# A hybrid decoder trunk: the first FFN by Strassen's method too, and the second layer's modulation on GpSimd

## The chip, the cores and the metric

The kernel runs on one core of one Trainium2 chip. The metric is the device time of one execution in microseconds; a figure for a kernel is the median of several runs. One execution is also taken by the hardware profiler, and its records are the trace that the sections below read. Five engines work side by side: TensorE (PE; PEld is its weight load), VectorE (DVE), ScalarE (ACT), GpSimd (POOL) and SyncE (SP), each with its own queue of instructions that it takes in order. They wait for each other by semaphores only.

## What is computed

A trunk of two residual layers over 512 tokens of 1024 channels, all in float32. Each layer has a mixer and a SwiGLU FFN, both behind an RMS norm that is shifted, scaled and gated by a modulation vector computed from `c`:

```python
h = x
c_act = silu(c)
for i in range(2):
    mod = c_act @ ada_w[i] + ada_b[i]              # 1024 x 6144, six parts of 1024
    sh_m, sc_m, gt_m, sh_f, sc_f, gt_f = split(mod, 6)
    hn = rms_norm(h, norm_mix_w[i]) * (1 + sc_m) + sh_m
    y = even_mixer(hn, ...) if i == 0 else odd_mixer(hn, ...)
    h = h + gt_m * y
    hn = rms_norm(h, norm_ffn_w[i]) * (1 + sc_f) + sh_f
    gate, up = split(hn @ ffn_w_in[i], 2)          # 1024 x 5632
    h = h + gt_f * ((silu(gate) * up) @ ffn_w_out[i])   # 2816 x 1024
return rms_norm(h, final_norm_w)
```

The even mixer is a gated DeltaNet beside an S5 state-space layer; the odd one is stick-breaking attention with eight heads.

## The kernel before

The activations stay in SBUF, channels on the partitions, 512 tokens along the free axis. Every weight is loaded by SyncE into one of two `raw` buffers, split into a high and a low part (ScalarE writes `whi`, L1535 and L1939; VectorE writes `wlo` = `raw` - `whi`, L2144), and multiplied in three passes (`pass3`, L622 to L624), high by high, high by low, low by high. A load of weights with its products is called a slot; slots alternate between the two buffers, so that a slot's `wlo` must be there before TensorE begins it.

**FFN of layer 0 (FFN0).** 2816 hidden channels are 22 tiles, in two halves of 12 and 10. A plain slot makes one tile: the gate block and the up block, 8 k-tiles by 3 passes each, 48 matmuls of 512 columns. ScalarE takes the Silu of the gate, VectorE multiplies (L2620) and splits into `ff_hi` and `ff_lo`. After each half eight out blocks multiply by `ffn_w_out`, and VectorE adds each, gated, to `h` (L2574).

**FFN of layer 1 (FFN1).** 22 tiles in thirds of 8, 8 and 6. The first four are plain slots, the other 18 Strassen slots: the tokens and the gate and up columns are each halved, and seven products of half the size (`half_product`, L1365 to L1367; 4 k-tiles by 3 passes, 256 columns) replace eight, 84 matmuls in all. VectorE makes sums of weight quarters for this (`sum_full`, L2830 to L2839, and their low part, L2847) and puts the corners together again (L2854, L2860, L2871). Four sums of activation quarters, the T tiles, are made once, before the first of these slots. Eight out blocks follow each third.

**The modulation.** Part p of layer i is `c_act @ ada_w[i]` over 1024 columns, taken as 8 tiles of 128 rows by 1024 columns: a tile is multiplied by one column of `c_act` (a scalar on each partition) and added to an accumulator. VectorE then folds the accumulator over the partitions in part, and TensorE ends it (`folded_parts`). Layer 0's fifth part (`scale_acc`) is done largely on GpSimd by a tensor_scalar (L3100) and a tensor_tensor (L3101) a tile, beside VectorE's products of the S5 output gate (`y_s`, L2519). Layer 0's last part, the FFN's gate, is 8 tiles on VectorE, two ahead of FFN0 and six within it. Layer 1's 48 tiles are done by VectorE within FFN0, three parts at a time, one scalar_tensor_tensor of 128x3072 behind a hidden tile (L2634), on loads that GpSimd's queue issues (L3121).

**What sets the order.** Nothing is scheduled by a program: each engine's instructions stand in the order in which the code is written, and the waits on semaphores do the rest. Between FFN0 and the attention stands `late_norm(2, ...)`, the norm of the attention's input; it needs the last out block, and TensorE's first product of the attention needs it.

Of the kernel before, what the change touches and what calls it, by code (L numbers as in the profile page):

```python
# [3159 lines left out]
```

## Time and profile before

| | |
|---|---|
| median of 3 runs | 1302.54 us (1300.65 to 1304.43) |
| the profiled execution's own time | 1305.82 us |
| its span, first to last instruction | 1304.2 us |
| mean granted TensorE clock, share of full speed | 0.986 |
| busy: PE, DVE, ACT, POOL | 1260.0, 864.0, 582.7, 181.0 us |

Busy time is an average over stages with different limits, so the stages are read one by one: FFN0 lies from about 349 to 699 us of the span, the norm behind it to 724, the attention to about 935, FFN1 to the end. A row of the timeline is one instruction, with its start and its duration; an engine that has to wait for another has in brackets how long it stood idle and what released it. An instruction whose operands are kept from it while it already runs has no such bracket: it is only longer.

### The profile page before, as it was taken

To read this page: it belongs to the slowest core of one execution; us is meant where nothing else is said; L and a number is where in the kernel's file an instruction comes from. 1 tells how busy PE (TensorE), PEld (TensorE's weight loads), DVE (VectorE), ACT (ScalarE), POOL (GpSimd) and SP (SyncE) were. 2 spreads that over 40 slices of the span, in tenths; PEclk is the share of its full clock that TensorE was granted. 3 is DMA by queue.
4 is the path that set the end of the run, shared out by engine and by line. 5 is a ranking of instruction groups with operands and counts; after the bars stand their busy time and mean duration, and the time that the engine had idled before them with its cause. 6 is when DMAs were issued, how large, how long until landed. Compare 5 with 4: busy or idle time off the path is not lost.

```text
span 1304.2 us, 19810 instructions
## 1 busy us (share of the span) xinstructions
PE 1260.0 (97%) x7915; PEld 1073.5 (82%) x7915; DVE 864.0 (66%) x1045; ACT 582.7 (45%) x747; POOL 181.0 (14%) x242
## 2 busy tenths in 40 slices
PE   5999999899999999999999999999999999999997
PEld 3588788788788888888888888887879989988995
DVE  3799976567876663466467466455789458846865
ACT  6444752444432222222334476556575335523543
POOL 4007964930000000000000000000500000000000
PEclk8999999989999999999999999999999999999999
DMA  9593625425248763377233221112232243325212
GB/s 338 160 145 122 188 76 154 140 86 173 66 122 286 232 222 105 112 241 240 59 90 129 97 65 65 57 57 81 65 97 82 80 126 101 97 75 146 83 59 90
DMA packets 207475, 163.34 MB, mean 125 GB/s; under 512 B 31790, under 2 KB 197899, under 8 KB 205355
## 3 DMA queue, kind: packets, MB, share of 16 engines
q1 hardware_dynamic: 204496, 137.02, 36.3%
q0 software_dynamic: 2400, 25.20, 5.3%
q8 instruction: 50, 0.82, 0.3%
q14 instruction: 23, 0.18, 0.0%
q10 hardware_dynamic: 506, 0.12, 0.0%
HBM read 157.21 MB, written 4.19 MB: 124 GB/s over the span
## 4 chain that ended last, share of the span: by engine, by line
PE 76%; DVE 9%; POOL 5%; ACT 5%; issue 2%; DMA 1%; ACTq 0%; POOLq 0%; DVEq 0%; SPq 0%
PE banks L622 17%; PE banks L624 17%; PE banks L623 17%; PE banks L1365 5%; PE banks L1367 5%; PE banks L1366 5%; DVE wlo L2144 2%; PE banks L937 2%; PE banks L1272 1%; PE banks L927 1%; PE banks L1234 1%; DVE hn_lo L2194 1%; POOL scan_a L3048 1%; DMA raw<-in_ffn_w_in_dram 1%; DVE tmp L2188 1%
## 5 line engine op out<-in xcount | busy, mean ns | idle before, releaser
L2144 DVE TENSOR_TENSOR wlo<-raw,whi 128x2048 fp32r<-128x2048 f32 (+4 forms) x116 | 229.1, 1976 | 87.5 <-ACT whi L1529 41.4
L622 PE MATMUL banks<-hn_hi,whi 128*128 128x512 f32 x688 | 273.8, 398 | 5.2 <-DVE hn_lo L2292 2.2
L624 PE MATMUL banks<-hn_hi,wlo 128*128 128x512 f32 x688 | 270.2, 393 | 0.0
L623 PE MATMUL banks<-hn_lo,whi 128*128 128x512 f32 x688 | 270.2, 393 | 0.0
L622 PE MATMUL banks<-ff_hi,whi 128*128 128x512 f32 x416 | 163.3, 392 | 0.0
L624 PE MATMUL banks<-ff_hi,wlo 128*128 128x512 f32 x416 | 162.0, 389 | 0.0
L623 PE MATMUL banks<-ff_lo,whi 128*128 128x512 f32 x416 | 162.0, 389 | 0.0
L622 PEld LDWEIGHTS banks<-hn_hi,whi 128*128 128x128 f32 x688 | 130.5, 190 | 36.0 <-DVE hn_lo L2194 3.5
L624 PEld LDWEIGHTS banks<-hn_hi,wlo 128*128 128x128 f32 x688 | 130.4, 190 | 27.7
L623 PEld LDWEIGHTS banks<-hn_lo,whi 128*128 128x128 f32 x688 | 130.7, 190 | 26.2
L1535 ACT ACTIVATE whi<-raw 128x2048 fp32r<-128x2048 f32 (+1 forms) x35 | 65.3, 1866 | 148.8 <-PE banks L624 148.8
L2574 DVE SCALAR_TENSOR_TENSOR h<-banks,mod,h 128x512 f32<-128x512 f32 x54 | 40.4, 748 | 87.7 <-PE banks L624 87.6
L624 PEld LDWEIGHTS banks<-ff_hi,wlo 128*128 128x128 f32 x416 | 78.1, 188 | 16.4
L623 PEld LDWEIGHTS banks<-ff_lo,whi 128*128 128x128 f32 x416 | 78.2, 188 | 15.8
L622 PEld LDWEIGHTS banks<-ff_hi,whi 128*128 128x128 f32 x416 | 78.1, 188 | 15.7
L1529 ACT ACTIVATE whi<-raw 128x2048 fp32r<-128x2048 f32 (+3 forms) x39 | 67.7, 1743 | 13.0 <-PE banks L624 13.0
L2634 DVE SCALAR_TENSOR_TENSOR ada_acc<-ada_in,c_act,ada_acc 128x3072 f32<-128x3072 f32 x16 | 54.6, 3412 | 0.7 <-DMA ada_in<-in_ada_w_dram 0.7
L3121 POOL DMA_DIRECT2D ada_in<-in_ada_w_dram x16 | 8.5, 533 | 326.2 <-DVE ada_acc L2634 209.4
L2620 DVE TENSOR_TENSOR tmp<-tmp,banks 128x512 f32<-128x512 f32 x21 | 14.5, 689 | 57.1 <-PE banks L624 55.3
L1939 ACT ACTIVATE whi<-raw 128x1024 fp32r<-128x1024 f32 (+1 forms) x24 | 23.6, 982 | 49.2 <-PE banks L624 49.2
L3127 POOL TENSOR_TENSOR shift_t<-raw,mod 128x2048 f32<-128x2048 f32 x1 | 3.6, 3602 | 300.1 <-DMA raw<-in_ffn_w_in_dram 300.1
L1365 PE MATMUL banks<-hn_hi,whi 128*128 128x256 f32 x144 | 40.9, 284 | 1.7 <-DVE wlo L2144 1.7
(569 smaller groups left out, 2647.0 us busy)
## 6 DMA issues: line engine op xcount, KB each, us to landing
raw<-in_ffn_w_in_dram SPq DMA_DIRECT2D x88, 512.0 KB, 4.9
ada_in<-in_ada_w_dram POOLq DMA_DIRECT2D x16, 1536.0 KB, 6.3
raw<-in_sb_w_in_dram SPq DMA_DIRECT2D x24, 512.0 KB, 4.4
raw<-in_hy_w_in_dram SPq DMA_DIRECT2D x20, 512.0 KB, 5.9
ada_in<-in_ada_w_dram SPq DMA_DIRECT2D x18, 512.0 KB, 4.4
ada_first<-in_ada_w_dram SPq DMA_DIRECT2D x8, 1024.0 KB, 15.0
raw<-in_ffn_w_out_dram SPq DMA_DIRECT2D x32, 256.0 KB, 3.1
raw<-in_ffn_w_out_dram SPq DMA_DIRECT2D x16, 384.0 KB, 4.0
```

What stands on the lines that cost most here:

```text
L622: pe.matmul(o, lh, rh, start=first, stop=False)
L623: pe.matmul(o, lh, rl, start=False, stop=False)
L624: return pe.matmul(o, ll, rh, start=False, stop=last)
L937: last = pe.matmul(bank[b][t:t + 64, 64 * c_:64 * c_ + 64], l(slice(t, t + 64), hd, c_), r(slice(t, t + 64), hd, c_), start=True, stop=True)
L1365: pe.matmul(o, wh[:, k, :], rh[:, k, :], start=first and k == 0, stop=False, skip_group_check=True)
L1366: pe.matmul(o, wh[:, k, :], rl[:, k, :], start=False, stop=False, skip_group_check=True)
L1367: last = pe.matmul(o, wl[:, k, :], rh[:, k, :], start=False, stop=k == 3, skip_group_check=True)
L1529: act.activation(whi[s][:, 0:width], raw[s][:, 0:width], ACT.Copy).then_inc(hi_done, 1)
L1535: act.activation(whi[s][:, 0:width], raw[s][:, 0:width], ACT.Copy).then_inc(hi_done, 1)
L2144: TTO(wlo[s][:, 0:width], raw[s][:, 0:width], whi[s][:, 0:width].bitcast(F32), SUB)\
L2574: STT(h[:, m, :], bank[b], mod[:, bass.ds(gate + m, 1)], h[:, m, :], MUL, ADD)\
L2634: STT(ada1_acc[:, :], ada1_in[s][:, :], c_act[:, bass.ds(ada_i * 2 + (s - 2), 1)], ada1_acc[:, :], MUL, ADD).then_inc(ada_used, 1)
```

## The change

FFN0 is computed by Strassen's method too, by the code that FFN1 had, now written once for both layers (`ffn(L)` on SyncE, TensorE, ScalarE and VectorE): four plain slots, 18 Strassen slots, thirds of 6, 8 and 8 in layer 0 and of 8, 8 and 6 in layer 1 as before. To make room, the fourth T tile is written into a quarter of `hn_hi` and `hn_lo` that the plain slots have read; ScalarE waits for plain slot 3 before it writes it.

The 48 modulation tiles of layer 1 go from VectorE to GpSimd: a tensor_scalar that multiplies the loaded tile in place, a tensor_tensor that adds it to the accumulator, and the issue of the load two tiles on. 32 tiles (four parts) are done from FFN0's T sums on, 16 (two parts) from the end of FFN0 on, within the attention. Two loads wait for weights: the sixth for those of the second third's first slot, the nineteenth for those of the last third's first slot; the 33rd waits for all blocks of FFN0. The first tile of a part waits until VectorE has folded the part before. VectorE's folds of the first four parts stand in fixed places of FFN0: behind the second Strassen slot of the second third, behind that third's first out block, behind the fourth Strassen slot of the last third, behind its fifth out block; those of the last two at the end of the attention's first and second pair of heads.

The gate's 8 tiles of layer 0 all stand ahead of FFN0 on VectorE, four while it waits for the mixer's out blocks and four between these; SyncE loads them in three pieces, the last behind a wait. SyncE loads the S5 output ahead of all `scale_acc` tiles.

```diff
-HALVES = (12, 10)
-FT = sum(HALVES)
+FT = 22
 PLAIN = 4
-THIRDS = (8, 8, 6)
+THIRDS = ((6, 8, 8), (8, 8, 6))
...
+        t_full, t_fourth = at("t_full", 174, [P, 3, 4, 256]), at("t_fourth", 186, [P, 4, 256])
+        ada1_in = [at(f"ada1_in{s}", o, [P, 1024]) for s, o in enumerate((152, 156))]
+        ada1_acc = at("ada1_acc", 186, [P, 1024])
...
@@ SyncE
             sp.wait_ge(o_done, NH)
-            for s in range(2):
-                sp.dma_start(gate_in[s][:, :, :], ada_w[0].rearrange("(p t) n -> p t n", t=8)[
-                    :, 4 * s:4 * s + 4, 5 * D:6 * D]).then_inc(gate_ld[s], 16)
+            gate_rows = ada_w[0].rearrange("(p t) n -> p t n", t=8)
+            sp.dma_start(gate_in[0][:, :, :], gate_rows[:, 0:4, 5 * D:6 * D]).then_inc(gate_ld[0], 16)
+            sp.dma_start(gate_in[1][:, :, :], gate_rows[:, 6:8, 5 * D:6 * D]).then_inc(gate_ld[1], 16)
+            sp.wait_ge(ada_used, 28)
+            sp.dma_start(gate_in[0][:, 2:4, :], gate_rows[:, 4:6, 5 * D:6 * D]).then_inc(gate_ld[0], 16)
...
@@ TensorE, for both layers now
+            def ffn(L):
+
+                first_pair(S_FF1 if L else S_FF0, IN_SLOT[L][0] * 2, 2 * L + 1, (0, 1), sums_at=2, rows_at=3 + L)
+                as_tiles_come(IN_SLOT[L][0] + 1, IN_SLOT[L][0] * 2 + 2, 2 * L + 1, (2, 3), halves)
+                plain_slot(L, 2)
+                plain_slot(L, 3, None if L else lambda: folded_parts(7, 5, 1, 2))
+                for t in range(3):
+                    with pe.Fori(0, len(strassen_of(L, t)) // 2) as i:
+                        for j in range(2):
+                            strassen_slot(L, t, i, j)
+                    for m in range(KT):
...
+                        out_block(L, t, m, between)
...
@@ ScalarE: the fourth T tile takes the place of a quarter of hn_hi
+            def t_rounded(L, n):
+
+                act.wait_ge(t_summed, after_one(4 * L + n + 1))
+                if n < 3:
+                    act.activation(t_hi[:, n], t_full[:, n], ACT.Copy).then_inc(t_hi_done, 1)
+                else:
+                    slot_left(act, IN_SLOT[L][0] + PLAIN - 1)
+                    act.activation(hn_hi[:, 0:4, 256:512], t_fourth[:, :, :], ACT.Copy).then_inc(t_hi_done, 1)
...
@@ VectorE
+            def ada1_fold(part):
+
+                dve.wait_ge(ada_used, 32 + 8 * (part + 1))
+                if part == 3:
+                    dve.wait_ge(mod_sum, 5)
+                fold((ada1_acc, ada2_acc)[part // 4], (0, 1, 0, 0, 1, 2)[part]).then_inc(c_ready, 1)
...
-                            if ada_i is not None:
-                                dve.wait_ge(ada1_ld[s], 64 * half + 16 * ada_i)
-                                dve.wait_ge(ada_used, 30 + 8 * half + s + 2 * ada_i)
-                                STT(ada1_acc[:, :], ada1_in[s][:, :], c_act[:, bass.ds(ada_i * 2 + (s - 2), 1)],
-                                    ada1_acc[:, :], MUL, ADD).then_inc(ada_used, 1)
...
+            FOLD_IN_SLOT = {(0, 1, 1): 0, (0, 2, 3): 2}
+            FOLD_IN_STAGE = {(0, 1, 0): 1, (0, 2, 4): 3}
...
@@ VectorE, attention
                 out_lo(a)
                 if p_ < 2:
+                    ada1_fold(4 + p_)
                     next_lo(p_ + 1, 2)
...
@@ GpSimd
-            pool.wait_ge(ada_used, 32)
-            for half in range(2):
-                with pool.Fori(1, 5) as i:
-                    for s in range(2):
-
-                        pool.wait_ge(ada_used, 29 + 8 * half + s + 2 * i)
-                        pool.wait_ge(block_done, B_FF0 + 2)
...
-                        pool.dma_start(ada1_in[s][:, :], src).then_inc(ada1_ld[s], 16)
+            def ada1_load(u):
+
+                part, t = u // 8, u % 8
+                if u == 5:
+                    pool.wait_ge(raw_in[IN_SLOT[0][1] % 2], 32 * (IN_SLOT[0][1] // 2 + 1))
+                elif u == 18:
+                    pool.wait_ge(raw_in[IN_SLOT[0][2] % 2], 32 * (IN_SLOT[0][2] // 2 + 1))
+                elif u == 32:
+                    pool.wait_ge(block_done, B_SB)
+                pool.dma_start((ada1_in if u < 32 else ada2_in)[u % 2][:, :],
+                               ada_w[1].rearrange("(p t) n -> p t n", t=8)[:, t, part * D:(part + 1) * D])\
+                    .then_inc(ada1_ld[u % 2], 16)
+
+            pool.wait_ge(t_summed, after_one(4))
+            ada1_load(0)
+            ada1_load(1)
+            for u in range(48):
+                part, t = u // 8, u % 8
+                in_, acc = (ada1_in[u % 2], ada1_acc) if u < 32 else (ada2_in[u % 2], ada2_acc)
+                pool.wait_ge(ada1_ld[u % 2], 16 * (u // 2 + 1))
+                if t == 0:
+                    if u > 0:
+                        pool.wait_ge(c_ready, 3 + part)
+                    else:
+                        pool.wait_ge(t_done, after_ada(4))
+                    pool.tensor_scalar(acc[:, :], in_[:, :], c_act[:, t:t + 1], None, MUL).then_inc(ada_used, 1)
+                else:
+                    step(pool.tensor_scalar(in_[:, :], in_[:, :], c_act[:, t:t + 1], None, MUL))
+                    pool.wait_ge(ada_used, 32 + u)
+                    pool.tensor_tensor(acc[:, :], acc[:, :], in_[:, :], ADD).then_inc(ada_used, 1)
+                if u == 31:
+                    ada1_load(32)
+                    ada1_load(33)
+                elif u < 46 and u != 30:
+                    pool.wait_ge(ada_used, 33 + u)
+                    ada1_load(u + 2)
```

VectorE in FFN0, the loop over the first half's hidden tiles before (one tile; `ada_in_74` is a piece of layer 1's `ada_w`, and a wait that stands in a row of its own belongs to the next instruction):

```order
L2620 TENSOR_TENSOR tmp_182<-tmp_181,banks 128x512 [waits block_free]
L2143 REGISTER_ALU
L2144 TENSOR_TENSOR wlo_54<-raw_50,whi_52 128x2048 [waits weights_hi_done]
L2623 ISA [waits hidden_hi]
L2623 TENSOR_TENSOR ff_lo<-tmp_182,ff_hi 128x512
L2632 REGISTER_ALU
L2633 ISA [waits ada1_loaded0]
L2634 ISA [waits ada_tiles_used]
L2634 SCALAR_TENSOR_TENSOR ada_acc<-ada_in_74,c_act,ada_acc 128x3072
```

VectorE in FFN0 after, the second Strassen slot of the second third with the fold behind it (`sum_full`, `raw` and `sum_lo` are weight sums; semaphores carry the names of their first users, so `ada_first3_loaded` counts weight sums here):

```order
L2568 TENSOR_TENSOR sum_full_68<-raw_50 128x512 [waits ada_first6_loaded,raw0_loaded]
L2592 TENSOR_TENSOR tmp_185<-banks,sq 128x512 [waits ada_first7_loaded,ada_first6_loaded]
L2572 TENSOR_TENSOR raw_50<-raw_50 128x512 [waits ada_first3_loaded]
L2573 TENSOR_TENSOR sum_full_68<-sum_full_68,raw_50 128x512
L2598 TENSOR_TENSOR banks<-diag 128x256 [waits ada_first7_loaded,block_done]
L2577 TENSOR_TENSOR sum_full_68<-sum_full_68,raw_50 128x512 [waits ada_first3_loaded]
L2606 SCALAR_TENSOR_TENSOR tmp_186<-banks,tmp_185 128x512 [waits block_free,ada_first0_loaded,gate_silu]
L2068 TENSOR_TENSOR wlo_54<-raw_50,whi_52 128x2048 [waits weights_hi_done]
L2534 TENSOR_TENSOR ff_lo<-tmp_186,ff_hi 128x512 [waits hidden_hi]
L2585 TENSOR_TENSOR sum_lo_66<-sum_full_68,sum_hi_64 128x1536 [waits ada_first4_loaded]
L1998 TENSOR_REDUCE mod_fold<-ada_acc 128x32 [waits ada_tiles_used]
```

The product of 128x512, the split of the weights and the 128x3072 of the modulation have become ten instructions on weights and corners, and the fold waits for GpSimd's tiles (`ada_tiles_used`).

GpSimd beside FFN0 before, the loop that issues layer 1's loads, behind its last tile work:

```order
L3110 TENSOR_TENSOR wlo_55<-raw_51,whi_53 128x2048 [waits weights_lo_done,weights_hi_done]
L3114 UNCONDITIONAL_BRANCH [waits ada_tiles_used]
L3114 ISA
L3121 ISA [waits block_done,ada_tiles_used]
L3121 DMA ada_in_74<-in_ada_w_dram 128x3072
L3117 REGISTER_ALU
L3121 ISA [waits block_done,ada_tiles_used]
L3121 DMA ada_in_75<-in_ada_w_dram 128x3072
L3114 REGISTER_ALU
L3114 COMPARE_AND_BRANCH
```

GpSimd beside FFN0 after, the third and fourth tile of the first part, the load behind each, of which the second is the sixth load, and the fifth tile (`ada_in_75` and `ada_in_76` are the two buffers, `raw0_loaded` is the arrival of weights):

```order
L3013 TENSOR_SCALAR ada_in_75<-ada_in_75,c_act 128x1024 [waits ada1_loaded0]
L3015 TENSOR_TENSOR ada_acc<-ada_acc,ada_in_75 128x1024 [waits ada_tiles_used,pool_steps]
L2995 DMA ada_in_75<-in_ada_w_dram 128x1024 [waits ada_tiles_used]
L3013 TENSOR_SCALAR ada_in_76<-ada_in_76,c_act 128x1024 [waits ada1_loaded1]
L3015 TENSOR_TENSOR ada_acc<-ada_acc,ada_in_76 128x1024 [waits ada_tiles_used,pool_steps]
L2995 DMA ada_in_76<-in_ada_w_dram 128x1024 [waits raw0_loaded,ada_tiles_used]
L3013 TENSOR_SCALAR ada_in_75<-ada_in_75,c_act 128x1024 [waits ada1_loaded0]
```

A loop of loads alone has become two arithmetic instructions and a load for each tile, and one of these loads stands behind the arrival of weights.

## Rows read from the trace of the kernel before

**Rows 1.** Windows: start:end and length, busy us of PE, PEld, DVE, ACT, POOL (instructions), clock, DMA share, GB/s.
```profile
352.00:470.00 118.00, 117.77 (x523) 96.19 (x522) 80.23 (x57) 37.38 (x39) 4.83 (x9) 1.00 0.62 200
1082.00:1132.00 50.00, 50.00 (x419) 50.00 (x418) 42.40 (x50) 29.21 (x45) 0.00 (x0) 1.00 0.34 95
741.00:787.00 46.00, 46.00 (x250) 38.61 (x249) 24.80 (x27) 29.98 (x28) 0.00 (x0) 1.00 0.25 79
700.00:723.00 23.00, 23.00 (x122) 18.75 (x121) 19.27 (x29) 12.68 (x16) 0.00 (x0) 1.00 0.25 85
```

**Rows 2.** Timeline (start, us, engine line op out<-in) of PE, FFN0, sixty matmuls apart.
```profile
363.61 0.39 PE L622 MATMUL banks<-hn_hi,whi 128*128 128x512 f32 x1
...
377.21 0.39 PE L622 MATMUL banks<-hn_hi,whi 128*128 128x512 f32 x1
```

**Rows 3.** Timeline of PE, FFN1, first matmuls of two Strassen slots.
```profile
986.78 0.28 PE L1365 MATMUL banks<-hn_hi,whi 128*128 128x256 f32 x1
...
996.86 0.28 PE L1365 MATMUL banks<-hn_hi,whi 128*128 128x256 f32 x1
```

**Rows 4.** Timeline of DVE in one Strassen slot of FFN1.
```profile
996.27 0.68 DVE L2830 TENSOR_TENSOR sum_full<-raw 128x512 f32<-128x512 f32 x1
996.87 0.68 DVE L2854 TENSOR_TENSOR tmp<-banks,sq 128x512 f32<-128x512 f32 x1
...
1000.42 2.29 DVE L2144 TENSOR_TENSOR wlo<-raw,whi 128x2048 fp32r<-128x2048 f32 x1
1003.69 0.69 DVE L2807 TENSOR_TENSOR ff_lo<-tmp,ff_hi 128x512 fp32r<-128x512 f32 x1 [0.98 <-ACT ff_hi L1954]
...
1005.96 0.68 DVE L2830 TENSOR_TENSOR sum_full<-raw 128x512 f32<-128x512 f32 x1
```

**Rows 5.** The page's groups: busy us, mean ns, idle before. Modulation in FFN0.
```profile
L2634 DVE SCALAR_TENSOR_TENSOR ada_acc<-ada_in,c_act,ada_acc 128x3072 f32<-128x3072 f32 x16 | 54.6, 3412 | 0.7 <-DMA ada_in<-in_ada_w_dram 0.7
L3121 POOL DMA_DIRECT2D ada_in<-in_ada_w_dram x16 | 8.5, 533 | 326.2 <-DVE ada_acc L2634 209.4
```

**Rows 6.** Timeline of POOL, tiles of layer 0's `scale_acc`.
```profile
227.83 2.85 POOL L3100 TENSOR_SCALAR scale_part<-scale_in,c_act 128x1024 f32<-128x1024 f32 x1
...
248.82 2.39 POOL L3101 TENSOR_TENSOR scale_acc<-scale_acc,scale_part 128x1024 f32<-128x1024 f32 x1
251.31 3.17 POOL L3100 TENSOR_SCALAR scale_part<-scale_in,c_act 128x1024 f32<-128x1024 f32 x1
254.56 2.40 POOL L3101 TENSOR_TENSOR scale_acc<-scale_acc,scale_part 128x1024 f32<-128x1024 f32 x1
257.06 3.16 POOL L3100 TENSOR_SCALAR scale_part<-scale_in,c_act 128x1024 f32<-128x1024 f32 x1
```

**Rows 7.** Timeline of DVE in the same stretch.
```profile
249.87 1.89 DVE L2519 TENSOR_TENSOR y_s<-y_s,tmp 128x512 f32<-128x512 f32 x1 [2.52 <-ACT tmp L1723]
252.59 0.70 DVE L2519 TENSOR_TENSOR y_s<-y_s,tmp 128x512 f32<-128x512 f32 x1 [0.83 <-ACT tmp L1723]
255.31 2.20 DVE L2519 TENSOR_TENSOR y_s<-y_s,tmp 128x512 f32<-128x512 f32 x1 [2.02 <-ACT tmp L1723]
258.03 1.01 DVE L2519 TENSOR_TENSOR y_s<-y_s,tmp 128x512 f32<-128x512 f32 x1 [0.52 <-ACT tmp L1723]
```

**Rows 8.** Timeline at FFN1's first boundary of thirds, DVE and PE.
```profile
1054.60 0.75 DVE L2574 SCALAR_TENSOR_TENSOR h<-banks,mod,h 128x512 f32<-128x512 f32 x1 [3.13 <-PE banks L624]
...
1070.42 0.39 PE L624 MATMUL banks<-ff_hi,wlo 128*128 128x512 f32 x1
1071.70 0.38 PE L1365 MATMUL banks<-hn_hi,whi 128*128 128x256 f32 x1 [0.90 <-DVE wlo L2144]
```

**Rows 9.** Timeline at the end of the norm ahead of the attention.
```profile
721.46 2.28 DVE L2144 TENSOR_TENSOR wlo<-raw,whi 128x2048 fp32r<-128x2048 f32 x1
...
723.80 0.39 PE L622 MATMUL banks<-whi,hn_hi 128*128 128x256 f32 x1
```

**Rows 10.** Windows, in the norm ahead of FFN1.
```profile
940.00:944.00 4.00, 4.00 (x19) 3.61 (x19) 2.88 (x8) 2.15 (x3) 0.00 (x0) 0.61 0.00 0
```

More of the change, by code:

```diff
@@ L588, in hidden_slot, with middle_slot @@
+            def middle_slot(L, n, tile):
                 b = n % 2
@@ L1192, in _, with plain_slot @@
-            ffn(0, 16, B_FF0, 1)
+            def plain_slot(L, j, between=None):
+                n = IN_SLOT[L][0] + j
+                slot_ready(n)
+                mh, ml = halves(whi[n % 2]), halves(wlo[n % 2])
+                for two in range(2):
+                    if j == 2:
+                        pe.wait_ge(pair_steps, pair_value(2 * L + 1, 1))
+                    else:
+                        pe.wait_ge(block_free, 2 * n + two - 3)
+                    for k in range(KT):
+                        last = pass3(bank[2 * (j % 2) + two][:, :], mh[:, k, two, :], ml[:, k, two, :],
+                                     hn_hi[:, k, :], hn_lo[:, k, :], k == 0, k == KT - 1)
+                        if between is not None and two == 1 and k == 5:
+                            between()
+                    last.then_inc(block_done, 1)
@@ new lines, in out_block @@
+            def out_block(L, t, m, between=None):
+                n, n_in = OUT_SLOT[L][t] + m, THIRDS[L][t]
+                mh, ml = (x_[n % 2][:, 0:n_in * P].rearrange("p (k m) -> p k m", k=n_in) for x_ in (whi, wlo))
+                slot_ready(n)
+                pe.wait_ge(block_free, 2 * n - 6 if m >= 4 else 2 * OUT_SLOT[L][t] - 2)
+                for k in range(n_in):
+                    if m == 0 and k == n_in - 1:
+                        pe.wait_ge(block_free, 2 * OUT_SLOT[L][t])
+                    last = pass3(bank[m % 4][:, :], mh[:, k, :], ml[:, k, :], ff1_hi[:, k, :], ff1_lo[:, k, :],
+                                 k == 0, k == n_in - 1)
+                    if between is not None and k == 1:
+                        between()
+                last.then_inc(block_done, 2)
@@ L1418, in _ @@
[L1418 to L1429 removed]
+            ffn(1)
@@ new lines, in sums_of, with first, second, third @@
+            def sums_of(q):
+                b = Q_SLOT[q] % 2
+                a11, a12, a21, a22 = (raw[b][:, 512 * n:512 * n + 512] for n in range(4))
+                s3, s2, s4 = (sum_full[q % 2][:, n, :] for n in range(3))
+                def first():
+                    dve.wait_ge(raw_in[b], 32 * (Q_SLOT[q] // 2 + 1))
+                    if q >= 2:
+                        dve.wait_ge(six, after_one(6 * (q - 2) + 6))
+                    TTO(s3, a11, a21, ADD).then_inc(w_sums, 1)
+                def second():
+                    dve.wait_ge(w_sums, after_one(4 * q + 1))
+                    TTO(a21, a21, a22, ADD).then_inc(w_sums, 1)
+                    TTO(s2, s3, a22, ADD).then_inc(w_sums, 1)
+                def third():
+                    dve.wait_ge(w_sums, after_one(4 * q + 3))
+                    TTO(s4, s2, a12, ADD).then_inc(w_sums, 1)
+                return first, second, third
```

1017 lines of the change are left out of this document (411 added, 606 removed).

## The prediction

> **What bounds the kernel now.** I read the windows by stage first, because an average over the span hides which engine sets the pace where. In FFN0's blocks, in FFN1's Strassen slots and in the attention TensorE is busy from end to end at granted clock 1.00, and VectorE is busy for 80 of 118 us, 42 of 50 us and 25 of 46 us [rows 1]. So TensorE sets the pace in all three, and VectorE is next: what makes VectorE's part of a slot longer than TensorE's makes the kernel longer. The normalization ahead of the attention is the one of these stretches where VectorE, 19.3 of 23 us busy, sets the end [rows 1].
>
> Then the timeline of TensorE gives the price of a hidden slot. A plain slot is 48 matmuls 512 wide; sixty of them lie between the two starts shown, 13.60 us, so one takes 0.2267 us and a slot 10.88 us [rows 2]. A Strassen slot is 84 matmuls 256 wide and starts every 10.08 us [rows 3].
>
> Third, VectorE's timeline inside one Strassen slot [rows 4]: ten instructions per slot, from `sum_full` to the next `sum_full` 9.69 us. By the distances of their starts the ten take 8.6 us, 0.98 us is a wait for ScalarE, and the rest are gaps. Eight of the ten read two operands in SBUF and make 7.3 us of the 8.6; two read a PSUM bank (`banks`) and make 1.3. `wlo`, which the next slot waits for, is done at 1002.71, and that slot begins at 1006.94: a lead of 4.2 us.
>
> **What the change adds for VectorE: GpSimd beside it.** In FFN0 before, GpSimd only issues loads, and VectorE does a layer-1 part with 16 instructions of 3412 ns [rows 5]. These 54.6 us go, but TensorE covered them; they are worth nothing by themselves. After, GpSimd does a tensor_scalar and a tensor_tensor of 128x1024 for each tile. Both exist before, in the tiles of `scale_acc`: 2.85 us and 2.39 us [rows 6], with a load's issue of 0.53 us [rows 5] and 0.1 us of gaps some 5.9 us a tile.
>
> What they do to VectorE is seen where the two meet. `y_s` is a 128x512 sum of two SBUF operands and takes 0.70 us when it runs free, as at 252.59 in the middle of GpSimd's tensor_scalar. Beside a tensor_tensor it took 1.89 and 2.20 us [rows 7]. Each time it ended about 0.55 us behind the tensor_tensor's end [rows 6]: 249.87 to 251.76 against an end at 251.21, and 255.31 to 257.51 against 256.96. So it ran only as the other finished, and the tensor_tensor keeps such an instruction out for some 2.25 of its 2.39 us. The tensor_scalar of 257.06 is itself held until 257.51, when `y_s` ends, and the next `y_s`, due at 258.03, ends 0.31 us late at 259.04, so it got in at 258.34: 0.85 us behind. The tensor_scalar thus keeps VectorE out for 0.85 us. That is 2.25 + 0.85 = 3.1 us per tile, and both ways: each waits for the other's current instruction.
>
> The Trainium skill, "SBUF — State Buffer", section "Who interferes with whom", says that a VectorE instruction with two SBUF inputs contends with a GpSimd instruction that reads SBUF, and that the shared ports are held for the whole instruction. The tensor_tensor rows agree; the tensor_scalar rows do not, since 0.70 us at 252.59 lies wholly inside one. By the page's letter a tile would cost 5.2 us of lock instead of 3.1; that is the third rival.
>
> **The price of a tile in a Strassen slot.** What reads two SBUF operands and GpSimd's holds exclude each other, so they add up: with two tiles in a slot 7.3 + 2 x 3.1 = 13.5 us. VectorE's wait and its PSUM reads fall under the holds; I take 13.6. GpSimd can do two tiles in that (2 x 5.9 = 11.8, and some 0.9 us of waiting for VectorE per tile). So a slot goes from 10.08 to 13.6 us and a tile costs 3.5 / 2 = 1.8 us. Lower bound: GpSimd never waits, 10.08 / 5.9 = 1.7 tiles in a slot, (7.3 + 1.7 x 3.1 - 10.08) / 1.7 = 1.5. Upper bound: it never waits in the longer slot either, 2.6 tiles, 2.1 us. What neither bound allows for is in the rivals.
>
> **The sum, against the profiled execution's 1305.8 us.**
> - Strassen in FFN0: 18 slots x (10.88 - 10.08) = -14.4.
> - Three thirds instead of two halves: at a boundary in FFN1 VectorE starts on the fourth block's `h` at 1054.60, with four 8-wide out blocks (16.3 us) ahead of TensorE, and TensorE waits 1.05 us for `wlo` [rows 8], a chain of 17.1 us. FFN0's first third is 6 wide, its four blocks are 12.2 us, and the chain, with smaller `wlo`, some 16.6: 4.4 us of wait there, 1.05 at the second. +5.5; bounds 0 (the one before, at its half boundary, costs as much) and 7.
> - GpSimd's tiles in FFN0. Their first loads wait for the T sums, the sixth for the weights of the second third, the nineteenth for those of the last, so few fall in the out blocks. First third: 4 tiles, 7.2 less the lead of 4.2, +3.0. Second: 11 in slots, 19.8 - 4.2, and 2.5 for the fold and for the last conversions at the boundary, +18.1. Last: 14, 25.2 - 4.2 + 2.5 = +23.5. Together +44.6; bounds 36 and 53 by the 1.5 and 2.1.
> - The normalization ahead of the attention: the first tiles of the attention's 16 are released by the last out block, and three fit into 23 us. 3 x 3.1 = 9.3 us of holds against VectorE's 3.7 us of idle time [rows 1, 9]. `wlo` of 721.46 ends just as TensorE's first normed matmul begins at 723.80 [rows 9], so a delay there goes straight to TensorE. Between 5.6 and 9.3; +7.5.
> - Attention: seven tiles fall on a pair of heads, 21.7 us of holds beside VectorE's 24.8 us of 46. That fills the pair, and the sums of a head wait some 3 us a pair: 2 x 3, and 1 for the last fold, which wants eight tiles by about 821 while GpSimd has them by 823 to 831. +7; bounds 0 (all beside TensorE's work) and 22 (half of the holds come through).
> - At nothing: the gate's tiles, now ahead of FFN0, lie in a wait of VectorE for TensorE and replace VectorE's own later tiles; the S5 loads' order; the fourth T tile, which waits for plain slot 3 but is wanted only by the fifth product of the slot after. TensorE covers them; without that cover 2 us each.
>
> 1305.8 - 14.4 + 5.5 + 44.6 + 7.5 + 7 = 1356.0 us. The profiled execution lies 3.3 us above the runs' median of 1302.5; off as much, 1353 us.
>
> **Rivals.**
> 1. GpSimd's holds cost nothing (the faster side): VectorE takes its operands first or the holds fall on its idle time and its PSUM reads, 2.8 us a slot. It decides if a tile holds VectorE for under 2.8 / 1.7 = 1.6 us instead of 3.1. For it: 0.98 us of waiting and 1.3 us on PSUM in each slot [rows 4]. Against: 1.89 and 2.20 us for work of 0.70 [rows 7]. 1305.8 - 14.4 + 5.5 - 3.3 = 1294 us.
> 2. GpSimd comes late at the folds: VectorE's short instructions win, and GpSimd gets only 2.8 us of free time a slot, 0.9 tiles. Then the fold after the second third's first out block is 3.5 tiles late and the one behind the fourth slot of the last third 2.4, at 5.9 us each 21 and 14, less the lead 17 and 10. For it: VectorE waits for these tiles in its own order. Against: `y_s` twice waited for GpSimd. With 3 for the normalization and 5 for the attention 1305.8 - 14.4 + 5.5 + 27 + 8 - 3.3 = 1329 us.
> 3. Both GpSimd instructions hold VectorE for all their time. Then each of its eight instructions stands behind one of GpSimd's, a slot is 7.3 + 4 x 5.2 = 28.1 us and a tile 4.5: 29 tiles are 131 - 12.6 + 5 = 123 instead of 44.6, some 1431 us. Against it stands 252.59 [rows 7].
> 4. The gain and the holds cancel (fewer tiles meet VectorE than I count): 1302.
>
> The granted clock is a matter of the upper end: TensorE now pauses 3.5 us in a slot, and a row shows 0.61 over 4 us in one place ahead of FFN1 [rows 10]. Half-speed stretches could add 15 us.
>
> **How the numbers follow.** The forecast 0.70, rival 1 0.14, rival 2 0.08, rival 3 0.05, rival 4 0.03. The forecast's own range is 1325 (tile at 1.5, attention and thirds at 0) to 1385 (tile at 2.1, attention at 22, some clock). To leave out no more than rivals 1 and 3 the range is 1300 to 1390. A measurement of this kernel tells about 0.3%, 3.9 us, from no change: faster 0.14, same 0.03, slower 0.83.
>
> **What would show it.** Right: first matmuls of FFN0's Strassen slots 13 to 14 us apart while GpSimd has tiles and 10.1 us apart once it has none, TensorE waiting for `wlo` or `sum_lo` of VectorE, VectorE's 128x512 sums at 1.9 to 2.9 us beside a tensor_tensor and at 0.7 beside a tensor_scalar, a tile of GpSimd every 6 to 7 us. Wrong: slots at 10.1 us with tiles beside them (rival 1), VectorE idle for GpSimd at the folds (rival 2), slots beyond 20 us (rival 3).

## The result and the profile after

The changed kernel takes 1364.47 us (median of 4 runs, 1363.05 to 1369.54); the kernel before, on the same chip, 1301.6 (1298.95 to 1304.43). The ratio is 1.0488, with a 95% interval of 1.0454 to 1.0522. The forecast was 1353, in a range of 1300 to 1390. The profiled execution took 1363.05 us, its span is 1361.3.

The two stages that the change touches, as windows (length, busy time of PE, PEld, DVE, ACT, POOL, clock, DMA share, GB/s): FFN0, then the norm with the attention. First the kernel before:

```profile
348.80:699.90 351.10, 350.72 (x1562) 288.42 (x1561) 214.18 (x168) 105.22 (x107) 8.53 (x16) 1.00 0.53 166
699.90:934.80 234.90, 232.64 (x1237) 194.07 (x1236) 132.71 (x144) 138.52 (x134) 17.25 (x9) 1.00 0.24 76
```

and the changed kernel:

```profile
344.20:733.60 389.40, 354.20 (x2209) 320.60 (x2207) 318.06 (x289) 162.62 (x235) 203.62 (x92) 0.96 0.44 128
733.60:994.70 261.10, 243.34 (x1246) 200.06 (x1246) 162.69 (x151) 138.68 (x134) 111.95 (x55) 0.96 0.32 101
```

FFN0 grew by 38.3 us, the norm and the attention by 26.2. The rest of the span became 7 us shorter, which other runs of the same code ahead of FFN0 and of FFN1 show to be spread: FFN0 begins between 343.6 and 350.0 us in the runs below.

TensorE was busy from end to end in both stages and now waits. Its waits (engine, line, waited for, us in total, times, longest), FFN0 and then norm and attention; before it had none in FFN0 and 2.2 us in the second stage:

```profile
PE banks L1127 <- ACT sq L1713: 22.8, 13, 3.7
PE banks L1127 <- DVE wlo L2068: 10.1, 2, 6.8
PE banks L601 <- DVE ff_lo L2534: 2.1, 1, 2.1
```

```profile
PE banks L1260 <- DVE later_lo L2737: 8.3, 2, 5.6
PE banks L601 <- DVE hn_lo L2118: 5.9, 5, 2.0
PE banks L1274 <- DVE w_b L2744: 1.5, 1, 1.5
PE banks L601 <- DVE wlo L2068: 1.1, 1, 1.1
```

These are 35 us and 17. The mean clock of 0.96 means that up to 0.04 x 389 = 16 us and 0.04 x 261 = 10 us more went to stretches at the lower of TensorE's two levels. Waits and clock account for TensorE's time: 17 - 2 + 10 = 25 of 26 us in the second stage, and in FFN0, with the 14.4 us that Strassen's slots save, 35 + 16 - 14 = 37 of 38. That says where TensorE's time went, not what set the pace. In the full slots and in the norm VectorE did, as the rows below show, and there the lower clock only stood in the place of more waiting.

What a slot looks like with two tiles beside it. VectorE from 492 us, the answer to [rows 4]:

```profile
491.67 1.75 DVE L2585 TENSOR_TENSOR sum_lo<-sum_full,sum_hi 128x1536 fp32r<-128x1536 f32 x1
493.34 1.60 DVE L2568 TENSOR_TENSOR sum_full<-raw 128x512 f32<-128x512 f32 x1
494.86 0.68 DVE L2592 TENSOR_TENSOR tmp<-banks,sq 128x512 f32<-128x512 f32 x1
495.46 0.68 DVE L2572 TENSOR_TENSOR raw<-raw 128x512 f32<-128x512 f32 x1
...
496.66 2.60 DVE L2598 TENSOR_TENSOR banks<-diag 128x256 f32<-128x256 f32 x1
...
500.38 2.81 DVE L2068 TENSOR_TENSOR wlo<-raw,whi 128x2048 fp32r<-128x2048 f32 x1
503.11 2.88 DVE L2534 TENSOR_TENSOR ff_lo<-tmp,ff_hi 128x512 fp32r<-128x512 f32 x1
505.92 1.74 DVE L2585 TENSOR_TENSOR sum_lo<-sum_full,sum_hi 128x1536 fp32r<-128x1536 f32 x1
```

GpSimd in the same stretch, the answer to [rows 6]:

```profile
492.15 3.98 POOL L3013 TENSOR_SCALAR ada_in<-ada_in,c_act 128x1024 f32<-128x1024 f32 x1
496.21 2.76 POOL L3015 TENSOR_TENSOR ada_acc<-ada_acc,ada_in 128x1024 f32<-128x1024 f32 x1
...
499.92 2.85 POOL L3013 TENSOR_SCALAR ada_in<-ada_in,c_act 128x1024 f32<-128x1024 f32 x1
502.86 2.59 POOL L3015 TENSOR_TENSOR ada_acc<-ada_acc,ada_in 128x1024 f32<-128x1024 f32 x1
```

No row of VectorE has a wait: from one `sum_lo` to the next it works or is kept out for 14.25 us. `ff_lo` and the 128x256 sum stand beside a tensor_tensor and are 2.2 us longer than free (0.68 and 0.42), `sum_full` and `wlo` beside a tensor_scalar 0.9 and 0.5 us. That is 5.8 us of holds on 8.6 of work. None of these holds is a wait on a semaphore: the held row is only longer. The same slot on TensorE, the answer to [rows 3], from its first matmul to the next slot's:

```profile
492.00 0.28 PE L1127 MATMUL banks<-hn_hi,whi 128*128 128x256 f32 x1
...
497.47 0.39 PE L1127 MATMUL banks<-t_hi,sum_hi 128*128 128x256 f32 x1 [2.43 <-ACT sq L1713]
...
506.25 0.28 PE L1127 MATMUL banks<-hn_hi,whi 128*128 128x256 f32 x1
```

and ScalarE, for which it waits:

```profile
495.57 0.63 ACT L1718 ACTIVATE tmp<-tmp 128x512 f32<-128x512 f32 x1 [5.87 <-DVE tmp L2592]
496.11 1.04 ACT L1694 ACTIVATE whi<-raw 128x1024 fp32r<-128x1024 f32 x1
497.06 0.36 ACT L1713 ACTIVATE sq<-banks 128x256 f32<-128x256 f32 x1
```

ScalarE's copy `sq` is small, but it stands in ScalarE's queue behind a Silu that waits for VectorE's sum `tmp`. So VectorE's lateness reaches TensorE through ScalarE, at the slot's third product.

### The profile page after: what moved, and what is told of

Same layout as the page of the kernel before. It is cut to its first block, busy times and chain, and to the rows that moved or that the text cites. A ratio compares the mean times of both kernels' runs of the same rounds, so it can differ in the third digit from the quotient of the medians.

```text
span 1361.3 us, 21229 instructions
## 1 busy us (share of the span) xinstructions
PE 1266.5 (93%) x8571; PEld 1105.1 (81%) x8571; DVE 1002.9 (74%) x1178; ACT 639.4 (47%) x875; POOL 471.2 (35%) x364
## 4 chain that ended last, share of the span: by engine, by line
PE 36%; DVE 8%; ACT 2%; issue 2%; DMA 1%; POOL 1%; DVEq 0%; SPq 0%; ACTq 0%; POOLq 0%
PE banks L601 6%; PE banks L603 6%; PE banks L602 6%; PE banks L1127 5%; PE banks L1129 5%; PE banks L1128 5%; DVE wlo L2068 2%; PE banks L1284 1%; DVE hn_lo L2118 1%; PE banks L1246 1%; DMA raw<-in_ffn_w_in_dram 1%; DVE tmp L2112 1%; POOL sq_sum L3037 1%; DVE hn_full L2112 0%; DVE e_b L2723 0%
## 5 line engine op out<-in xcount | busy, mean ns | idle before, releaser
L2068 DVE TENSOR_TENSOR wlo<-raw,whi 128x2048 fp32r<-128x2048 f32 (+3 forms) x124 | 239.3, 1930 | 52.9 <-ACT whi L1461 34.0
L601 PE MATMUL banks<-hn_hi,whi 128*128 128x512 f32 x400 | 162.7, 407 | 12.0 <-DVE hn_lo L2118 6.6
L602 PE MATMUL banks<-hn_lo,whi 128*128 128x512 f32 x400 | 158.4, 396 | 0.0
L603 PE MATMUL banks<-hn_hi,wlo 128*128 128x512 f32 x400 | 158.2, 395 | 0.0
L3013 POOL TENSOR_SCALAR ada_in<-ada_in,c_act 128x1024 f32<-128x1024 f32 x42 | 138.3, 3294 | 1.8
L3015 POOL TENSOR_TENSOR ada_acc<-ada_acc,ada_in 128x1024 f32<-128x1024 f32 x42 | 113.7, 2707 | 3.5
L601 PEld LDWEIGHTS banks<-hn_hi,whi 128*128 128x128 f32 x400 | 76.6, 192 | 34.2 <-DVE hn_lo L2118 11.8
L601 PEld LDWEIGHTS banks<-ff_hi,whi 128*128 128x128 f32 x416 | 78.5, 189 | 18.7 <-DVE ff_lo L2534 2.5
L602 PEld LDWEIGHTS banks<-ff_lo,whi 128*128 128x128 f32 x416 | 78.5, 189 | 15.7
L1128 PE MATMUL banks<-hn_lo,whi 128*128 128x256 f32 x288 | 84.2, 292 | 0.0
L1129 PE MATMUL banks<-hn_hi,wlo 128*128 128x256 f32 x288 | 83.9, 291 | 0.0
L1127 PE MATMUL banks<-hn_hi,sum_hi 128*128 128x256 f32 x288 | 81.7, 284 | 1.0 <-ACT sq L1713 1.0
```

The source lines that it names most:

```text
L601: pe.matmul(o, lh, rh, start=first, stop=False)
L602: pe.matmul(o, lh, rl, start=False, stop=False)
L603: return pe.matmul(o, ll, rh, start=False, stop=last)
L1127: pe.matmul(o, wh[:, k, :], rh[:, k, :], start=first and k == 0, stop=False, skip_group_check=True)
L1128: pe.matmul(o, wh[:, k, :], rl[:, k, :], start=False, stop=False, skip_group_check=True)
L1129: last = pe.matmul(o, wl[:, k, :], rh[:, k, :], start=False, stop=k == 3, skip_group_check=True)
```

## Experiments

Each run has the kernel before beside it. In e1 to e4 and in e8 the modulation of layer 1 is left out in part. Stage lengths are read from TensorE's timeline of each profile: FFN0 from its first product to its last out block, then to the attention's last out block. The changed kernel's rise over "no arithmetic" is what the tiles on GpSimd cost.

| kernel | median us | ratio to before (95%) | FFN0 us | norm and attention us |
|---|---|---|---|---|
| before | 1301.6 | | 351.0 | 235.0 |
| changed | 1364.5 | 1.0488 (1.0454 to 1.0522) | 389.4 | 261.1 |
| e1 no arithmetic | 1296.9 | 0.9969 (0.9950 to 0.9988) | 346.5 | 236.6 |
| e2 none in FFN0 | 1327.1 | 1.0213 (1.0180 to 1.0246) | 346.5 | 262.3 |
| e3 tensor_scalar alone | 1313.3 | 1.0090 (1.0060 to 1.0121) | 355.6 | 241.0 |
| e4 tensor_tensor alone | 1347.7 | 1.0372 (1.0335 to 1.0410) | 379.5 | 254.5 |
| e8 memset | 1297.2 | 0.9981 (0.9970 to 0.9992) | 347.3 | 236.4 |
| e9 plain FFN0, tiles on GpSimd | 1355.6 | 1.0447 (1.0404 to 1.0489) | 405.6 | 235.0 |
| e5 no load waits | 1358.6 | 1.0452 (1.0431 to 1.0474) | 382.8 | 262.5 |
| e10 after the norm | 1359.3 | 1.0450 (1.0432 to 1.0467) | 390.0 | 257.3 |
| e6 thirds 8, 8, 6 | 1366.8 | 1.0495 (1.0452 to 1.0539) | 381.6 | 269.1 |
| e7 tiles on VectorE | 1311.7 | 1.0083 (1.0050 to 1.0115) | 361.3 | 236.3 |
| e11 the same, 8, 8, 6 | 1309.6 | 1.0058 (1.0035 to 1.0081) | 354.5 | 238.9 |
| e12 the same, spread | 1300.1 | 0.9977 (0.9957 to 0.9997) | 345.0 | 241.0 |

**e1 and e2: is it GpSimd's arithmetic, and where?**

```diff
-                    step(pool.tensor_scalar(in_[:, :], in_[:, :], c_act[:, t:t + 1], None, MUL))
+                    step(pool.tensor_scalar(in_[:, 0:32], in_[:, 0:32], c_act[:, t:t + 1], None, MUL))
...
-                    pool.tensor_tensor(acc[:, :], acc[:, :], in_[:, :], ADD).then_inc(ada_used, 1)
+                    pool.tensor_tensor(acc[:, 0:32], acc[:, 0:32], in_[:, 0:32], ADD).then_inc(ada_used, 1)
```

(e2: `0:32 if u < 32 else 1024`.)

> The changed kernel with GpSimd's tensor_scalar and tensor_tensor cut to 32 of 1024 columns in 42 of the 48 tiles (the modulation of layer 1 is thus not computed in full); loads, waits, folds and order stay. Theory (the holds): nearly all of the rise goes. FFN0's 389 us fall to about 341 (335 of work and some 6 at the boundaries), the norm and the attention to within 2 us of before: some 1290 us. Rival (FFN0's Strassen form and its third boundary cost the time, GpSimd little): over 1340 us. Rival (the loads and their waits): unchanged, 1364.

> As the run before, but only the 32 tiles of FFN0 are cut; the attention's 16 stay whole. Theory: FFN0 at some 341 us, norm and attention at 26 us above before: about 1316 us. If the attention's rise followed from FFN0's (a late start, a lower clock), norm and attention would fall too and the time be near 1292.

Without arithmetic the kernel is 68 us faster than changed and 0.3% faster than before: the whole rise is GpSimd's arithmetic. FFN0's length follows its 32 tiles (42.9 us) and the second stage its own 16 (24.5 to 25.7), the one independent of the other. e1's FFN0 as a window (columns as above):

```profile
343.60:690.10 346.50, 338.90 (x2209) 308.84 (x2208) 250.49 (x289) 162.75 (x235) 83.35 (x92) 1.00 0.48 144
```

VectorE has the same 289 instructions there as in the changed kernel and is busy for 250 us instead of 318. FFN0 was 5 us longer than expected, 346.5: TensorE still waits 4.5 and 1.0 us for `wlo` at the boundaries, and the slot behind the longer wait takes 11.7 us.

**e3, e4 and e8: which instruction holds?** One of e1's two edits each; e8 cuts the tensor_scalar and puts a memset in place of the tensor_tensor:

```diff
-                    pool.tensor_tensor(acc[:, :], acc[:, :], in_[:, :], ADD).then_inc(ada_used, 1)
+                    pool.memset(in_[:, :], 0.0).then_inc(ada_used, 1)
```

> The changed kernel with only the tensor_tensor cut to 32 columns, the tensor_scalar whole (part of the modulation is left out). Theory (a tensor_scalar holds VectorE for 0.5 to 0.9 us of its 2.85): Strassen slots with tiles at 10.8 to 11.3 us, about 1302 us. Rival (it holds for its whole time): slots beyond 14 us, over 1335 us.

> The changed kernel with only the tensor_scalar cut to 32 columns, the tensor_tensor whole (part of the modulation is left out). Theory (a tensor_tensor holds VectorE for 2.2 us of its 2.4): three a slot instead of two, slots of 14 to 16 us, but the tiles are through sooner; most of the rise stays, about 1345 us. Rival (both kinds hold alike): as much as with the tensor_scalar alone.

> The changed kernel with the tensor_scalar cut to 32 columns and the tensor_tensor replaced by a memset of 1024 columns of the loaded tile (the modulation is left out): GpSimd writes SBUF and reads next to nothing. If only a GpSimd instruction that reads SBUF keeps VectorE's second operand out, FFN0 stays at the 346 us that it has without arithmetic, about 1297 us. If any GpSimd instruction does, each of 42 memsets (some 1 us) costs, slots with three of them would be at 11.5 us and more, about 1315 us.

Over e1's FFN0 the tensor_scalar adds 9.1 us, the tensor_tensor 33.0, together 42.1 of the 42.9. Slots with a tensor_scalar alone are 10.5 to 10.9 us (the first of a third 12.6 and 11.6), with a tensor_tensor alone up to 15.7; the time with the tensor_scalar alone is 11 us above what was expected, mostly by e1's 5 and by 4.4 in the attention. In e4 VectorE's sums beside a tensor_tensor again take 2.87 us, and the tensor_scalar of 32 columns waits for VectorE's `wlo` in turn. VectorE, then GpSimd:

```profile
486.79 2.87 DVE L2568 TENSOR_TENSOR sum_full<-raw 128x512 f32<-128x512 f32 x1
...
495.15 4.34 DVE L2068 TENSOR_TENSOR wlo<-raw,whi 128x2048 fp32r<-128x2048 f32 x1
```

```profile
485.42 3.69 POOL L3015 TENSOR_TENSOR ada_acc<-ada_acc,ada_in 128x1024 f32<-128x1024 f32 x1
...
498.29 1.95 POOL L3013 TENSOR_SCALAR ada_in<-ada_in,c_act 128x32 f32<-128x32 f32 x1
```

The memset costs nothing that shows: FFN0 347.3 against 346.5, VectorE's sum at 0.68 us beside it. e8's VectorE and GpSimd:

```profile
480.39 0.68 DVE L2572 TENSOR_TENSOR raw<-raw 128x512 f32<-128x512 f32 x1
```

```profile
480.08 0.95 POOL L3015 MEMSET ada_in<- 128x1024 f32 x1
```

**e9: the same tiles beside plain slots.** In the kernel before, GpSimd does the 48 tiles on the 3072-wide loads; the core of the edit:

```diff
-                                STT(ada1_acc[:, :], ada1_in[s][:, :], c_act[:, bass.ds(ada_i * 2 + (s - 2), 1)],
-                                    ada1_acc[:, :], MUL, ADD).then_inc(ada_used, 1)
...
+                for n in range(3):
+                    c_ = slice(n * D, (n + 1) * D)
+                    in_, acc = ada1_in[u % 2][:, c_], ada1_acc[:, c_]
...
+                        step(pool.tensor_scalar(in_, in_, c_act[:, t:t + 1], None, MUL))
+                        pool.wait_ge(ada_used, 32 + u)
+                        last = pool.tensor_tensor(acc, acc, in_, ADD)
```

> The kernel before (FFN0 by plain slots, VectorE at 4 us of work in a slot of 10.9) with the 48 tiles of layer 1 done by GpSimd in FFN0, as 128x1024 tensor_scalars and tensor_tensors on the 128x3072 loads; VectorE's 128x3072 instructions are gone. Theory: the holds fall on VectorE's idle time, FFN0 stays within 4 us of 351, about 1302 us. Rival (GpSimd's arithmetic costs wherever it stands): 40 us more, 1340 us.

The time was expected wrongly, 1355.6 us, and neither theory's reason made it. TensorE's only long wait in FFN0 is one:

```profile
PE banks L737 <- DVE mod_fold L2092: 53.0, 1, 53.0
```

GpSimd begins its tiles behind the gate's, needs about 140 us for the first 24 (396 to 535 us), and the fold stands fixed in VectorE's queue ahead of that. Beside plain slots it costs nothing, as the theory has it: windows of e9 with GpSimd at work for 97% and 87% of the time (columns as above):

```profile
405.00:468.00 63.00, 63.00 (x280) 52.18 (x279) 31.73 (x17) 16.05 (x17) 61.05 (x24) 1.00 0.56 173
560.00:697.00 137.00, 137.00 (x606) 113.49 (x605) 62.97 (x37) 34.73 (x32) 119.14 (x43) 1.00 0.50 154
```

TensorE has no idle time, at full clock. The 405.6 us of FFN0 less 53.0 are 352.6, against 351.0 before. So in the slots Strassen's sums, which fill VectorE, and GpSimd's tiles, which keep it out, cost only together.

**e5, e10 and e6: is it the placing?** e5 takes the two load waits out; e10 holds the attention's loads until the norm is over; e6 changes the thirds:

```diff
-                if u == 5:
-                    pool.wait_ge(raw_in[IN_SLOT[0][1] % 2], 32 * (IN_SLOT[0][1] // 2 + 1))
-                elif u == 18:
-                    pool.wait_ge(raw_in[IN_SLOT[0][2] % 2], 32 * (IN_SLOT[0][2] // 2 + 1))
-                elif u == 32:
+                if u == 32:
```

```diff
-                    pool.wait_ge(block_done, B_SB)
+                    pool.wait_ge(hn_done, 8 * 3)
```

```diff
-THIRDS = ((6, 8, 8), (8, 8, 6))
+THIRDS = ((8, 8, 6), (8, 8, 6))
```

> The changed kernel without the two loads' waits for weights. Theory (a tile costs in the slots and little in the out blocks, where VectorE has idle time): tiles 4 to 7 and 17 to 23 move into the out blocks; the first slots of the second and of the last third fall from 11 to 15.5 us toward 10.1, the waits at the boundaries by 2 to 3 us: FFN0 from 389 to some 377 us, about 1352 us. Rival (the waits keep the modulation's loads off the weights' loads): TensorE waits for weights' loads at the boundaries and the time stays or rises.

> The changed kernel with the attention's first loads of tiles waiting for the norm's last hn_lo instead of FFN0's last block. Theory: the norm's 13 us of rise go (the tensor_tensors no longer stand between its scalar_tensor_tensors, TensorE doesn't pause, and its clock stays), the last two folds come no later than they do: norm and attention from 261 to some 249 us, about 1352 us. Rival: the tiles cost the same wherever they stand in the attention: 1362.

> The changed kernel with FFN0's thirds 8, 8 and 6 instead of 6, 8 and 8, all tiles on GpSimd as changed. Theory: the first out blocks are a third longer, so at the first boundary TensorE waits some 3 us instead of 6.8; the last 15 tiles meet 6 slots instead of 8 and end in the out blocks, where they cost less: about 1357 us. Rival (VectorE's chain at the boundary doesn't end later than TensorE's blocks): same as changed, 1364.

All three gave half of what was expected, or none. e5: FFN0 6.6 us shorter instead of 12; the first boundary's wait stayed (6.4 us) and the second's rose from 3.3 to 5.3, since the tiles now stand beside the conversions of the out blocks (the last `wlo` of 128x768 there takes 3.10 us instead of 0.96). By the medians it gains 6 us, though the intervals overlap. e10: the norm takes 24.8 us instead of 36.8, the gain that was expected, but the attention 8.2 more, since its first pair of heads now has tiles too; the sums' waits rose from 8.3 to

```profile
PE banks L1260 <- DVE later_lo L2737: 13.7, 4, 5.5
```

so the two together gained 4 us, not 12. e6: FFN0 7.8 us shorter, norm and attention 8.0 longer, with 5.3 us of waits for `wlo` ahead of the attention behind the now shorter last out blocks. Moved tiles meet VectorE at the next full place.

**e7, e11 and e12: the tiles back on VectorE.** GpSimd only loads; VectorE does a tile in one instruction:

```diff
+            def ada1_tiles(n):
+
+                for _ in range(n):
...
+                    dve.wait_ge(ada1_ld[u % 2], 16 * (u // 2 + 1))
...
+                        STT(acc[:, :], in_[:, :], c_act[:, t:t + 1], acc[:, :], MUL, ADD).then_inc(ada_used, 1)
...
                         lo(slot + 1, (slot + 1) % 2, n_in * P if last else 2048)
+                        if L == 0 and t > 0:
+                            ada1_tiles(1)
```

e11 adds e6's edit; e12 spreads the tiles:

```diff
-                        if L == 0 and t > 0:
+                        if L == 0 and (t > 0 or before):
...
-            TILES_IN_STAGE = {(0, 0, 0): 2, (0, 0, 1): 2, (0, 0, 2): 2, (0, 0, 3): 2,
-                              (0, 1, 1): 3, (0, 1, 2): 3, (0, 1, 3): 2, (0, 2, 0): 1, (0, 2, 1): 1}
+            TILES_IN_STAGE = {(0, 0, 0): 2, (0, 0, 1): 1, (0, 0, 2): 1, (0, 0, 3): 1,
+                              (0, 1, 1): 2, (0, 1, 2): 1, (0, 1, 3): 1, (0, 1, 4): 1,
+                              (0, 2, 0): 2, (0, 2, 1): 1, (0, 2, 2): 1, (0, 2, 3): 1}
```

> The changed kernel with the 48 tiles back on VectorE, one tensor_scalar or scalar_tensor_tensor of 128x1024 a tile (1.3 us), GpSimd only issuing loads: 8 in the first third's out blocks, 8 in the second third's slots, 8 in its out blocks, 8 in the last third's slots, 16 in the attention's first two pairs of heads, folds moved to fit; no waits of loads for weights. Theory: with no GpSimd arithmetic nothing is held, 8.6 + 1.3 us fit into a slot of 10.08: FFN0 some 348 us, norm and attention 238, about 1299 us, 60 us below the changed kernel and 2 below before. Rival (VectorE has no room for a tile in a slot): slots of 11 us and more, 1315 us.

> As the run before with thirds of 8, 8 and 6 in FFN0 (two tiles of the last part go to its out blocks). Theory: at the first boundary TensorE waits 1 us for VectorE instead of 4.5 and its clock stays, 5 us less: about 1294 us, faster than before by 0.5%. Rival (the wait moves on to another boundary or to the loads): the same time as the run before.

> As the run before (tiles on VectorE, thirds of 8, 8 and 6), with the tiles spread so that two buffers of loads keep up: one per Strassen slot in all three thirds, else one per out block (two in the first). In the run before VectorE waited 14 us for the tiles' loads and TensorE 15 us for wlo at out blocks with two and three tiles, while every slot with one tile ran at 10.08 us. Theory: these waits go to some 3 us, FFN0 from 354.6 to about 343 us, 1298 us, a little below before. Rival (what TensorE waits for is VectorE's arithmetic, not the loads): 1308 us.

In e7 every slot with a tile ran at 10.08 us, the first of each third apart (12.2 and 10.2), but the bunches of two and three in the out blocks waited for loads (16 us of VectorE's waits are for `ada_in`), and TensorE for VectorE's `wlo` behind them; e11 missed likewise. Spread, VectorE does the tile within the slot:

```profile
490.12 2.29 DVE L2088 TENSOR_TENSOR wlo<-raw,whi 128x2048 fp32r<-128x2048 f32 x1
492.33 1.28 DVE L2059 SCALAR_TENSOR_TENSOR ada_acc<-ada_in,c_act,ada_acc 128x1024 f32<-128x1024 f32 x1
493.79 0.69 DVE L2554 TENSOR_TENSOR ff_lo<-tmp,ff_hi 128x512 fp32r<-128x512 f32 x1 [0.17 <-ACT ff_hi L1723]
```

FFN0 is 345.0 us, 6 below before and 44 below changed. The whole is 0.9977 of before (0.9957 to 0.9997): the fastest here that computes everything, by a hair, since norm and attention took 6 us more than before, 3.6 of them one wait for `wlo` behind the short out blocks.

## Why the prediction was right, and where it was short

- **Direction and mechanism** held: slots at 14.25 us with two tiles (13.6 forecast), VectorE's sums at 2.8 to 2.9 us beside a tensor_tensor, 10.1 once GpSimd is done, a tile every 7.1 us. Within a tensor_scalar they took 0.68 us, as forecast, except the one that met its beginning (`sum_full`, 1.60). The medians rose by 62.9 us; 50.2 were forecast.
- **GpSimd's tiles in FFN0**: forecast +44.6, measured 42.9 (changed against e1). That this came so close is in part luck, since two errors offset each other: by thirds, each taken up to the first slot of the next, the tiles cost 6.5, 18.1 and 18.4 us where 3.0, 18.1 and 23.5 were forecast. In the first third the out blocks took 4.0 us more than in e1 and the wait at the boundary 2.3 more, 6.8 us. Why the last third was cheaper than forecast stays open.
- **The slot** was short by 0.65 us. The holds of two tiles were 5.8 us, less than the forecast 2 x 3.1, but nothing of them fell under VectorE's wait or its PSUM reads: VectorE's queue simply became one chain.
- **Strassen and the thirds**: -14.4 + 5.5 = -8.9 forecast; e1 against before gives -4.5. The 4.4 us at the first boundary was 4.5. Missing are a slow slot behind the boundary (1.6), the first Strassen slot, in which the fourth T tile is written (1.2, costed at nothing), and two slots behind a fold (0.7 each).
- **Two slips** in the working changed nothing: the 16.3 and 12.2 us ahead of TensorE at a boundary are three out blocks, not four, and the forecast's own lower end adds up to about 1332, not 1325.
- **Norm and attention**: forecast +14.5, measured +26, 12.9 in the norm and 13.3 in the attention. In the norm the price of a tile, 3.1 us, came out (12 us for four); the step that failed is "three fit into 23 us". The holds lengthen the norm, and in its 36.8 us GpSimd does five tiles, four of them with a tensor_tensor. The norm before, in the changed kernel and in e2 (columns as above):

```profile
699.90:723.80 23.90, 23.77 (x124) 19.05 (x122) 20.06 (x29) 13.37 (x18) 0.00 (x0) 1.00 0.25 83
733.60:770.40 36.80, 29.43 (x125) 21.51 (x124) 34.10 (x33) 14.26 (x19) 30.31 (x17) 0.86 0.47 145
695.80:732.60 36.80, 27.19 (x125) 20.04 (x125) 34.07 (x34) 15.52 (x19) 30.36 (x17) 0.95 0.46 145
```

  In the changed kernel VectorE's rows from `diag` (L2106, 739.65 us) to the end of `wlo` take 30.7 us instead of 18.7 (705.09 to 723.74 before), with 0.2 us of idle time, and TensorE's first product of the attention waits for that `wlo`:

```profile
746.71 2.88 DVE L2118 SCALAR_TENSOR_TENSOR hn_lo<-tmp,mod,hn_hi 128x512 fp32r<-128x512 f32 x1
...
751.57 0.74 DVE L2118 SCALAR_TENSOR_TENSOR hn_lo<-tmp,mod,hn_hi 128x512 fp32r<-128x512 f32 x1
...
765.90 4.46 DVE L2068 TENSOR_TENSOR wlo<-raw,whi 128x2048 fp32r<-128x2048 f32 x1
770.42 0.38 PE L601 MATMUL banks<-whi,hn_hi 128*128 128x256 f32 x1 [1.11 <-DVE wlo L2068]
```

  The clock fell here too. After several waits of 1 to 2 us for VectorE, 10 of 11 us went at TensorE's lower level:

```profile
757.00:768.00 11.00, 9.31 (x22) 6.20 (x22) 10.61 (x9) 3.39 (x5) 10.49 (x5) 0.53 0.33 96
```

  But it did not lengthen the norm: e2's is as long at a clock of 0.95 as this one at 0.86, because VectorE sets its end. In the attention the forecast was seven tiles and 3 us for each of two pairs of heads. The first pair, which begins at 787.5 us, cost nothing: the first eight tiles were done by 789.2, and GpSimd then waited 33.7 us for VectorE's fold:

```profile
823.77 2.84 POOL L3011 TENSOR_SCALAR ada_acc<-ada_in,c_act 128x1024 f32<-128x1024 f32 x1 [33.68 <-DVE mod_fold L1998]
```

  All eight tiles of the last part so fell on the second pair, which took 58.8 us instead of 46.0 (before, then changed):

```profile
786.80:832.80 46.00, 46.00 (x250) 38.56 (x249) 24.80 (x27) 28.70 (x27) 0.00 (x0) 1.00 0.21 70
833.50:892.30 58.80, 50.53 (x249) 41.97 (x248) 40.06 (x28) 28.95 (x27) 36.95 (x17) 0.91 0.32 99
```

- **How it reaches TensorE**: I named `wlo` and `sum_lo`. `wlo` it was at the boundaries only; in the slots it was ScalarE's copy behind the Silu (22.8 of 35 us).
- **Rivals**: 1 (no cost) fell by e1; 2 (late folds) did not happen here, but it is what e9 met; 3, where each GpSimd instruction holds all its time, falls by e3: a tensor_scalar costs a fifth of the whole, not half; 4 (gain and holds cancel) falls by the time itself. The Trainium skill, "SBUF — State Buffer", section "Who interferes with whom", has the two-operand case right, and that GpSimd's writing alone doesn't contend is borne out by e8. A hold for the whole instruction, as the prediction cites it, the rows do not show for a tensor_scalar: it kept such instructions out for 0.5 to 0.9 of its 2.85 us.

What stays open is how much the lower clock costs by itself elsewhere. Of FFN0's 16 us some 10 lie in the six slots of 14 us and more (86.9 us at a clock of 0.88); VectorE has no idle time in these, so there the clock adds nothing. For the other 6 and for up to 5 in the attention's second pair (0.09 x 58.8) no run tells.

## What to carry to other kernels

An engine with idle time is no free room when its instructions keep out those of the engine that is next in line: price a moved instruction by how long it keeps the other out, and look at how full that other engine is in that stage, not over the span. Count the instructions over the stage as they lengthen it, not over the stage as it was. Two changes that each cost nothing in the slots (Strassen's extra sums on VectorE, tiles on GpSimd) can cost 43 us together. When TensorE waits in short pieces and its clock falls, see which engine ends the stage before adding the clock to the sum.
